# Two transformer blocks on one core: where the mLSTM gates' functions stand, and how the first operands reach the chip

## The reference

```
def layer_norm(x, g, b):
    mu = jnp.mean(xf, axis=-1, keepdims=True)
    xc = xf - mu
    var = jnp.mean(xc * xc, axis=-1, keepdims=True)
    y = xc * lax.rsqrt(var + LN_EPS)
    return y * g + b

def mlstm_post(h, o_pre, z, head_g):
    h = jax.nn.sigmoid(o_pre) * h
    hh = rmsnorm(h.reshape(B, T, M_HEADS, M_HEAD_DIM), head_g.reshape(M_HEADS, M_HEAD_DIM))
    return hh.reshape(B, T, M_WIDTH) * jax.nn.silu(z)

    out_x = jnp.concatenate([att_x, m_x], axis=-1) @ w_out
    x = x + gate_x * out_x
```

## Time and profile before

| | us |
|---|---|
| time, median of 3 runs | 2094.78 (2093.93 to 2096.22) |
| the profiled execution, its own time | 2075.97 |
| span of its profile, first to last instruction | 2073.8 |
| PE busy in the span | 2014.3 (97%) |
| DVE busy | 783.8 (38%) |
| ACT busy | 412.4 (20%) |

### The profile page before, as it was taken

The page is one execution under the profiler, slowest core; times in us unless marked ns, Lnnn a source line. Parts: engine busy times, 40 slices in busy tenths (PEclk is TensorE's granted clock), DMA queues, the critical chain, the costliest instruction groups (busy, mean ns, idle before and its releaser), DMA issues.

```text
span 2073.8 us, 36617 instructions
## 1 busy us (share of the span) xinstructions
PE 2014.3 (97%) x15746; PEld 1457.6 (70%) x15746; DVE 783.8 (38%) x1776; ACT 412.4 (20%) x970; POOL 5.8 (0%) x12
## 2 busy tenths in 40 slices
PE   8999999999999999999999999999899999999997
PEld 6869999987776666666666666556765668466786
DVE  5836555577341120111111111011415745435664
ACT  1233211013330112000010000000214443223332
POOL 0000000000000000000000000000000000000000
PEclk9999999999999999999999999999999999999999
DMA  9483444445259999999999999999221111122120
GB/s 323 164 294 121 177 178 168 175 188 209 75 228 371 420 418 415 421 420 420 420 420 420 420 421 420 420 415 415 100 101 61 41 61 42 61 102 82 62 82 21
DMA packets 72370, 506.72 MB, mean 244 GB/s; under 512 B 7824, under 2 KB 9872, under 8 KB 11792
## 3 DMA queue, kind: packets, MB, share of 16 engines
q1 hardware_dynamic: 71056, 500.15, 60.0%
q0 software_dynamic: 1152, 4.19, 0.9%
HBM read 503.27 MB, written 1.05 MB: 243 GB/s over the span
## 4 chain that ended last, share of the span: by engine, by line
PE 90%; DMA 4%; DVE 2%; ACT 2%; issue 1%; DVEq 0%; SPq 0%; ACTq 0%
PE ps L456 88%; DMA ring<-weights 2%; DMA work<-weights 2%; PE ps L1195 1%; PE ps L748 1%; DMA xc<-x_t 0%; PE ps L1252 0%; PE ps L623 0%; DVE work L2747 0%; DVE work L2013 0%; PE ps L1296 0%; ACT work L1861 0%; DVE work L2019 0%; ACT work L1589 0%; ACT work L1852 0%
## 5 line engine op out<-in xcount | busy, mean ns | idle before, releaser
L456 PE MATMUL ps<-work 128*32 128x256 f32 (+8 forms) x5200 | 559.9, 379 | 9.0 <-DMA work<-weights 3.5
L456 PE MATMUL ps<-work,ring 128*128 128x256 f32 (+2 forms) x2024 | 510.4, 407 | 7.4 <-DVE work L2747 5.0
L456 PEld LDWEIGHTS ps<-work 128*32 128x32 f32 (+3 forms) x5200 | 364.8, 140 | 146.2 <-issue 76.0
L456 PE MATMUL ps<-ring,work 128*32 128x256 f32 (+3 forms) x5216 | 444.1, 411 | 11.3 <-DMA ring<-weights 4.6
L456 PEld LDWEIGHTS ps<-work,ring 128*128 128x128 f32 x2024 | 346.2, 191 | 142.5 <-issue 106.9
L456 PEld LDWEIGHTS ps<-ring,work 128*32 128x32 f32 (+1 forms) x5216 | 251.1, 119 | 172.1 <-issue 89.3
L456 PE MATMUL ps<-xc,ring 128*128 128x256 f32 (+1 forms) x1440 | 276.0, 352 | 2.9 <-DVE xc L2037 1.6
L456 PEld LDWEIGHTS ps<-xc,ring 128*128 128x128 f32 x1440 | 241.7, 191 | 40.1 <-issue 7.5
L2289 DVE TENSOR_TENSOR work<-work,ps 128x256 f32<-128x256 f32 x42 | 17.7, 421 | 418.2 <-ACT work L1662 418.2
L456 PE MATMUL ps<-xc,work 128*128 128x256 f32 (+1 forms) x720 | 138.1, 350 | 0.0
L456 PEld LDWEIGHTS ps<-xc,work 128*128 128x128 f32 x720 | 121.0, 191 | 18.4 <-issue 2.9
(11 more groups left out here) (278 smaller groups left out, 1217.1 us busy)
## 6 DMA issues: line engine op xcount, KB each, us to landing
ring<-weights SPq DMA_DIRECT2D x316, 1024.0 KB, 11.4
work<-weights SPq DMA_DIRECT2D x155, 1024.0 KB, 16.1
work<-rel POOLq DMA_DIRECT2D x8, 512.0 KB, 9.6
con<-consts SPq DMA_DIRECT2D x1, 1368.0 KB, 21.5
xc<-x_t SPq DMA_DIRECT2D x1, 1024.0 KB, 7.4
xc<-ctx_t SPq DMA_DIRECT2D x1, 1024.0 KB, 25.3
out<-work SPq DMA_DIRECT2D x4, 256.0 KB, 2.1
par<-params SPq DMA_DIRECT2D x1, 872.0 KB, 8.8
```

What stands on the lines that cost most here:

```text
L456: ins = eng.matmul(o, lhs, rhs, start=start, stop=stop, **kw)
```

## The change

At the start, the ones are written on the chip by a DVE memset, PE spins ten times over 128 columns of them, x is loaded in two halves ahead of the constants, and ACT makes one square of the ones ahead of the first norm. In the second block, `mo` is projected ahead of `mz`. ACT takes the sigmoid inside the scan, behind step 17; the silu stands behind step 20 in layer 1 and behind the square root in layer 0. DVE gates, squares and sums tiles 2 and 3 of layer 0 inside the scan (at j = 3), and the other tiles behind it. The transposes of layer 0 stand between chunks 1 and 2 of the started output projection, in two halves with a signal each; those of layer 1 stay behind all four chunks.

```
-UNITS_IN2 = ["aq", "aq", "ak", "vg", "az", "az", "mk", "mk", "mq", "mq", "mv", "mv", "mz", "mz", "mo", "mo"]
+UNITS_IN2 = ["aq", "aq", "ak", "vg", "az", "az", "mk", "mk", "mq", "mq", "mv", "mv", "mo", "mo", "mz", "mz"]
...
+        POST_TILES = ([[2, 3], [0, 1]], [[0, 1]])
+        SIGMOID_AT, SILU_AT = 17, {1: 20}
...
+                    elif c % X_CHUNKS == 0:
+                        eng.wait_ge(x_in[c // X_CHUNKS], 16)
                     last = mm(o[:, 0:n], ones, src[:, c, 0:n], c == 0, c == chunks - 1)
...
+                for u in range(2):
+                    w = next_unit()
+                    for t in range(q_tiles):
+                        b = 7 if u or t or l else 6
+                        o = fill(("mo", l, u, t), b, (s["mo_copied"], 8 * l + q_tiles * u + t + 1))
+                        yield from token_pieces(("mo", l, u, t), w, t, o, b)
                 for c in range(M_HEADS):
...
+                    o = fill(("mz", l, c), 7, (s["mz_copied"], 4 * l + c + 1))
+                    yield from feature_pieces(("mz", l, c), w, (c % 2) * P, o, n_q, 7)
...
             def mlstm_turn(l):
-                eng.wait_ge(s["mh_normed"], l + 1)
-                for t in range(4 if l == 0 else 2):
...
+                for k, own in enumerate(POST_TILES[l]):
+                    eng.wait_ge(s["mh_normed"], normed_no(l, k))
+                    for i, t in enumerate(own):
...
                 for c in range(4):
+                    if l == 0 and c == 2:
+                        mlstm_turn(l)
...
+                if l:
+                    mlstm_turn(l)
                 return started
...
-            eng.wait_ge(s["ones_loaded"], 16)
-            spin(2)
-            eng.wait_ge(s["x_loaded"], 16)
+            eng.wait_ge(s["ones_ready"], 1)
+            spin(10, P)
             norm("in", xc, KC, T)
-            spin(3)
+            eng.wait_ge(s["early_loaded"], 16)
+            spin(3, 512)
...
-            eng.dma_start(con[:, 0:CN.early], consts[:, 0:CN.early]).then_inc(s["ones_loaded"], 16)
-            eng.dma_start(xc[:, :, 0:T], x_t).then_inc(s["x_loaded"], 16)
+            for i in range(X_PARTS):
+                own = slice(X_CHUNKS * i, X_CHUNKS * (i + 1))
+                eng.dma_start(xc[:, own, 0:T], x_t[:, own, :]).then_inc(x_in[i], 16)
+            eng.dma_start(con[:, P:CN.early], consts[:, P:CN.early]).then_inc(s["early_loaded"], 16)
...
                     copies_until(copies, waiting, n + 1)
+                    if n == SIGMOID_AT:
...
+                        eng.wait_ge(s["mo_copied"], 8 * l + 2 * q_tiles)
+                        eng.activation(mos[:, 0:q_tiles, :], mos[:, 0:q_tiles, :], ACT.Sigmoid)\
+                            .then_inc(s["mos_out"], 1)
+                    if n == SILU_AT.get(l):
...
+                        mlstm_silu(l)
...
-            eng.wait_ge(s["ones_loaded"], 16)
-            norm("in", KC, T)
+            eng.wait_ge(s["ones_ready"], 1)
+            eng.activation(std1[:, 0:P], ones, ACT.Square)
+            norm_squares("in", KC, T)
+            eng.wait_ge(s["early_loaded"], 16)
+            norm_std("in", KC, T)
...
                 mlstm_std(l)
+                if l not in SILU_AT:
+                    mlstm_silu(l)
...
+            def gated_heads(l, k):
+
+                first, end = POST_TILES[l][k][0], POST_TILES[l][k][-1] + 1
+                h2, o2 = (v[:, first:end, :].rearrange("p a b -> p (a b)") for v in (hs, mos))
+                o3 = mos[:, first:end, :].rearrange("p a (b c) -> p (a b) c", c=M_DH)
+                eng.wait_ge(s["mos_out"], l + 1)
+                link(eng.tensor_tensor(h2, h2, o2, ALU.mult))
+                link(eng.tensor_tensor(o2, h2, h2, ALU.mult))
+                return eng.tensor_reduce(rms_s[:, first * M_HEADS:end * M_HEADS], o3, AX.X, ALU.add)
...
+                    if l == 0 and j == 3:
+                        link(gated_heads(l, 0))
...
+                gated_heads(l, 1 - l).then_inc(s["mh_sumsq"], 1)
                 eng.wait_ge(s["mh_std"], l + 1)
                 link(eng.reciprocal(rms_i[:, 0:n], rms_i[:, 0:n]))
...
+                for own in POST_TILES[l]:
...
+                    eng.tensor_tensor(h3, h3, inv.broadcast_to([P, 2 * M_HEADS, M_DH]), ALU.mult)\
+                        .then_inc(s["mh_normed"], 1)
...
-            eng.wait_ge(s["x_loaded"], 16)
+            eng.memset(ones, 1.0).then_inc(s["ones_ready"], 1)
```

More of the change, by code:

```diff
@@ L72 @@
 EARLY_GATES = 2
+X_PARTS = 2
 GATE_CELLS = [3, 7]
@@ L328, in build @@
         weights_in = [ctx.enter_context(nc.semaphore(f"weights_in{i}")) for i in range(MOE_SLOTS)]
+        x_in = [ctx.enter_context(nc.semaphore(f"x_in{i}")) for i in range(X_PARTS)]
         late_in = [ctx.enter_context(nc.semaphore(f"late_in{i}")) for i in range(3)]
@@ L333, in build @@
         N_LATE = 3
+        X_CHUNKS = KC // X_PARTS
         RING = ring_places()
@@ L460, in mm, with spin @@
                 return ins
-            def spin(n):
+            def spin(n, cols):
                 for _ in range(n):
-                    mm(ps[:, 7, :], ones, con[:, 0:512], True, True)
+                    mm(ps[:, 7, 0:cols], ones, con[:, 0:cols], True, True)
             def norm(name, src, chunks, n, centred=True, bank=0):
@@ L1439, in _ @@
                 started = block2_out_start(l)
-                mlstm_turn(l)
                 block2_out(l, started)
@@ L1784, in block2_third @@
                             value_copy(l, u, t)
-                for c in range(M_HEADS):
-                    yield "mz", l, c
-                    o = tile(eng, "mz", l, c)
-                    eng.activation(mzs[:, c, 0:n_q], o[:, 0:n_q], ACT.Copy).then_inc(s["mz_copied"], 1)
                 for u in range(2):
@@ L1794, in block2_third @@
                             .then_inc(s["mo_copied"], 1)
+                for c in range(M_HEADS):
+                    yield "mz", l, c
+                    o = tile(eng, "mz", l, c)
+                    eng.activation(mzs[:, c, 0:n_q], o[:, 0:n_q], ACT.Copy).then_inc(s["mz_copied"], 1)
                 if l == 1:
```

47 lines of the change are left out of this document (17 added, 30 removed).

## The result

| | before | changed |
|---|---|---|
| median, 20 runs each | 2093.51 us | 2082.32 us |
| lowest to highest | 2075.96 to 2102.83 | 2070.54 to 2089.91 |
| profiled execution: time, span, mean granted clock | 2075.97, 2073.8, 0.995 | 2070.54, 2068.5, 0.995 |

The ratio is 0.995 (95% interval 0.9932 to 0.9968): 11.2 us faster, where 6.4 were predicted, and 2082.32 lies outside the range of 2086.0 to 2092.0. The two profiled executions differ by 5.4 us, though, and in them most of the steps can be seen as predicted. Runs of one kernel lie up to 27 us apart. The 2088.4 of the prediction came off 2094.78, a median of three runs; the twenty of the table have 2093.51, so 1.3 us of its miss stand there.

What follows compares the result with a forecast made beforehand. TensorE, busy for 97% of the span, bounds the kernel, so only its waits or half-clock time can move it. Terms 2.9 + 0 + 2.3 + 0 + 1.2 = 6.4 us saved: median 2088.4 us, range 2086.0 to 2092.0.

Steps and rivals of the forecast that it cites:

- The start, 2.9: Kernel start: x loaded ahead of the constants lets the mean end at 9.41, not 12.35; 2.9 us saved, between 2.3 and 3.1.
- The clock, 1.2: Behind layer 1's transposes: PE's clock no longer falls during the last 64 passes; 1.2 us saved, between 0 and 1.6.
- x lands at 7.55: Kernel start: landing time taken for x's second half, the middle between 6.95 and 8.2 us.
- the early bound of 6.95: Kernel start: x's landing time in us if x and the constants had flowed evenly from 0.77 to 8.6.
- The table load: Kernel start: ACT's first load leaves the path, the second comes onto it, 1.28 us each; net 0.
- that rival: ACT's table switches take 1.38 us longer than the load, at both exposed switches: 3.6 us saved, 2091.2; chance 0.08.
- Layer 0, 2.3: End of layer 0's scan: PE's 3.09 us idle go, one new tile-change wait costs 0.73; 2.3 us saved.
- Layer 1, 0: Layer 1's scan and transposes: idle time ahead of the transposes moves into the scan; nothing saved.
- The wait: Layer 1's scan: PE waits 1.5 us for ACT's scaled copies behind the sigmoid, replacing 1.70 us idle ahead of the transposes.
- the rival: Layer 1, behind the transposes: PE's clock falls all the same; 1.2 us less, 5.2 saved, 2089.6; chance 0.16.
- The narrow spin: Kernel start, rival: the 128-column spin doesn't bring PE to its upper clock; 3.0 us saved, 2091.8; chance 0.09.
- Every change of tile waits: Both layers' scans, rival: every bank 7 tile change waits 0.73 us; 5.7 us slower, 2100.5; chance 0.04.

Runs made afterwards that it cites:

- The start alone: The kernel before with only the edits at its start, both layers of the second block as before: 2085.41 us, ratio 0.9965.
- the filling: Spin passes of 256 and 512 columns in PE's idle time in each layer's neighbourhood attention, added to several kernels: before 2078.75 us, changed 2071.57 us.
- the layers' edits: The changed kernel with the start of the kernel before, so only the second block's edits: 2089.02 us, ratio 0.9976.

## Why the prediction was wrong

The step that failed is the one in which one execution stood for all: "Nothing in the profile says where the difference lies; I take the sum from the profiled execution and subtract it from the median as well." That execution of before had none of the long stretches and, of the five profiles of the old start, the earliest rise of the clock. One term of the sum, the start, was mis-sized by it, and probably a second, the clock.

- **The start, 2.9.** At one clock the change saves 7.8 us, where the prediction's terms other than the clock make 5.2 (2.9 + 0 + 2.3 + 0). The recorded clock begins with its first rise, so what a late first rise costs counts here. The layers have their part (2.7 against 2.3). The start alone gives 5.3 there, 4.2 with the filling, and 4.1 (+- 0.6) by the beginnings of the projection in the traces.
- **The clock, 1.2.** The runs show 2.6, with an error of 1.3, so 1.2 isn't excluded by them. The traces have 1.6 behind layer 1's transposes, and 1.3 in layer 0 and 0.4 lost at the start, which the prediction put at nothing.

7.8 and 2.6 make 10.4; what the medians have more, 0.8, lies within the scatter of twenty runs.

The 18.8 us between the two figures of before were mostly long stretches at the lower clock, which come or not from execution to execution, and each median holds a sample of them. Over all measurements before's 124 runs have a mean of 2092.6 and the changed kernel's 32 one of 2082.4, 10.2 apart. Against the means with the filling (2078.6 and 2071.4, 7.2 apart) the stretches cost 14.0 and 11.0 us. The 3 us between these have an error of 1.6. Whether they are chance, or the change makes the stretches rarer, stays open. The range held the bounds of the costs and nothing for this scatter.

Term by term:

- **Start, 2.9: too small.** In six profiles the new start's projection begins at 18.83 on the mean, in five of the old one at 22.93: 4.1 earlier, not 2.9, since the old start's clock often rises late. In four of the six, the clock falls behind the 2.41 us that the exposed table load leaves idle, which I hadn't foreseen: 0.4 to 0.8 us are given back each time, 0.4 on the mean. So 3.7 is left. That x lands at 7.55 was too late a guess: by 7.35 both halves were there, and in one piece x landed at 6.58, ahead of the early bound of 6.95.
- **The table load: right.** It moved onto the path, and the load itself costs 1.28, with 0.02 between it and its neighbours. The Trainium skill (ScalarE: Activation LUTs, What ACT_TABLE_LOAD costs) has 1.38 us of drain on top; by these rows of ACT there is none, and that rival falls.
- **Layer 0, 2.3: right.** In every profile with the layers' edits the segment is 2.4 shorter. (The sum's own figures give that: 3.09 less 0.73 is 2.36; and eight passes at 8.80 / 40 take 1.76, not 1.73.) Missing was the clock, a term put at nothing: behind the 3.09 us it stayed at 1.00 in the profile that I had, but it fell in three of the five kernels that keep this idle time (1.7, 1.7 and 3.0 us lost, 1.3 on the mean). I took one execution's clock for a rule.
- **Layer 1, 0, and its clock, 1.2.** The wait moved as told, and next to nothing is gained. It is 1.22 and not 1.5; the prediction's own times, 2024.4 less 2023.06, make 1.3. The clock gained more: it fell behind the transposes in all six kernels with the gates' functions behind the scan and in none of ten with the sigmoid at step 17, 1.6 in the rows above. With the sigmoid at step 14 it fell in three of three, so the rival was near; what decides between these places isn't settled. The Trainium skill (TensorE: Matmul & The Clock Gate, Part 4: PE-mode transpose) says that transposes don't count as busy; ten executions without a fall behind these transposes and nine with one neither bear that out nor refute it.
- **The rivals.** The narrow spin did bring PE to its upper clock; without it 1.5 to 2.8 us are lost. "Every change of tile waits" didn't come: one new wait, 0.63 us.

The terms as the traces have them (3.7, 2.4, 1.3, and 1.75 for the end of layer 1) make 9.2. That is 2 us more than the 7.2 +- 0.9 with the filling, and 1 less than the 10.2 +- 1.3 of the means without it. Some of it goes again in short falls elsewhere: near 166 the clock fell, for 1.7 us of time, in four of the six profiles with the new start and in one of the five with the old. That may be chance.

## What to carry to other kernels

A median less a profiled execution's time is a quantity to be explained, not a constant: ask first which runs the profile belongs to, read each term from several executions, compare runs at one granted clock, and measure a change of some microseconds with what scatters the runs taken away. Short idle times of PE between narrow matmuls can cost far more than themselves, so filling them with passes that compute nothing may gain more than taking a wait off the path. Where a table load depends on nothing, look for what stands ahead of it in its engine's list.

## What the hardware showed that I had not expected

Behind two idle times of 0.59 and 0.99 us PE's clock fell for 10 to 41 us, in which PE was busy throughout; 1.8 us of passes in these places, in each layer, took this away in eight profiles of eight, and 14 us off the mean of the kernel before. The Trainium skill (TensorE: Matmul & The Clock Gate, A second HAM failure mode: psum-queue depth-cycling) tells of short idle times between groups of matmuls that send the clock back and forth; here it went down once and stayed there, at the same two places, in most executions but not in all. The first upper clock of the same start came anywhere between 6.6 and 13.3 us.
